# Attention on one Trainium2 core: the local heads' tiles move in between the steps of the branch and latent tiles, with two output banks open at a time

## The reference, cut to what matters

```python
h = rms_norm(x, g_pre);  projections = h @ w_in                 # 22 tiles of 128 columns
# 4 heads, three branches each, gated and added up:
o_a = g0 * attend(q, compressed k, v; 31 keys)                  # "cmp"
    + g1 * attend(q, selected k, v; causal)                     # "slc": all 8 blocks are chosen, so all earlier keys
    + g2 * attend(q, windowed k, v; causal, window 512)         # "win"
# 4 latent heads, query and key width 64 + 32 (rope), causal:
o_b = attend(q_full, k_full, v)                                 # "mla"
# 8 local heads, window 128, one key head, a sink in the softmax:
o_c = attend(q, k, v; window 128)                               # "swa"
mixed = concat(o_a, o_b, o_c) * silu(z)                         # 256 + 256 + 512 = 1024 columns: 8 tiles of 128
x = x + rms_norm(mixed @ w_out, g_post)
```

## Time and profile before

| | us |
|---|---|
| median of three runs (lowest to highest) | 2488.43 (2487.45 to 2489.74) |
| the profiled execution's own time | 2487.56 |
| its span in the profile | 2485.8 |
| PE busy in the span | 2422.5 (97%) |
| DVE busy | 1292.6 (52%) |
| ACT busy | 659.6 (27%) |
| POOL busy | 644.2 (26%) |
| first layer's steps on PE from step 3 to the output projection | 163.37 to 246.37 |
| the same in the second layer | 446.91 to 529.83 |

### The profile page before, as it was taken

How to read it: one execution, slowest core, us unless ns; L and a number is a source line. 1 busy time by engine, 2 the same in 40 slices (tenths; PEclk the granted TensorE clock), 3 DMA queues, 4 the chain that set the end, 5 groups by cost and what they waited for, 6 DMA issues and landing times. The chain is left out here.

```text
span 2485.8 us, 35391 instructions
## 1 busy us (share of the span) xinstructions
PE 2422.5 (97%) x13586; PEld 1982.0 (80%) x13586; DVE 1292.6 (52%) x1969; ACT 659.6 (27%) x1364; POOL 644.2 (26%) x509
## 2 busy tenths in 40 slices
PE   8999999999999999998999999999999998999997
PEld 6777777677888888887888888888888887888886
DVE  6558575665333446877333345333445967433344
ACT  3047311652111005443111103111104453211102
POOL 2027300463333111004333213333112004333211
PEclk9999999999999999999999999999999999999999
DMA  5210222012223321212222322223331202222322
GB/s 207 97 61 19 100 102 77 27 60 68 97 97 101 104 92 69 95 52 77 93 98 96 118 90 69 101 93 101 105 98 68 100 30 85 94 100 93 120 93 80
DMA packets 58144, 219.07 MB, mean 88 GB/s; under 512 B 6392, under 2 KB 9608, under 8 KB 57776
## 3 DMA queue, kind: packets, MB, share of 16 engines
q1 hardware_dynamic: 55312, 206.87, 24.4%
q10 hardware_dynamic: 2720, 10.66, 1.1%
HBM read 215.38 MB, written 2.13 MB: 87 GB/s over the span
## 5 line engine op out<-in xcount | busy, mean ns | idle before, releaser
L180 DVE CAST two_hi<-two_raw 128x1024 fp32r<-128x1024 f32 (+1 forms) x291 | 217.8, 748 | 891.9 <-PE bank L248 872.4
L241 PE MATMUL bank<-xh,two_hi 128*128 128x512 f32 x1712 | 425.8, 391 | 0.0
L244 PE MATMUL bank<-xh,two_lo 128*128 128x512 f32 x1712 | 423.0, 389 | 0.0
L248 PE MATMUL bank<-xl,two_hi 128*128 128x512 f32 x1712 | 422.9, 389 | 0.0
L182 DVE TENSOR_TENSOR two_lo<-two_raw,two_hi 128x1024 fp32r<-128x1024 f32 (+1 forms) x291 | 404.1, 1389 | 9.9
L244 PEld LDWEIGHTS bank<-xh,two_lo 128*128 128x128 f32 x1712 | 321.6, 188 | 66.7
L248 PEld LDWEIGHTS bank<-xl,two_hi 128*128 128x128 f32 x1712 | 321.6, 188 | 66.5
L241 PEld LDWEIGHTS bank<-xh,two_hi 128*128 128x128 f32 x1712 | 320.2, 188 | 67.3 <-issue 1.0
L1829 POOL TENSOR_TENSOR hm<-sg,hm 128x512 f32<-128x512 f32 x88 | 193.6, 2200 | 552.5 <-ACT hm L1806 552.5
L1806 ACT ACTIVATE hm<-bank 128x512 f32<-128x512 f32 x88 | 52.9, 601 | 416.1 <-PE bank L248 413.4
L241 PE MATMUL bank<-hh,two_hi 128*128 128x512 f32 x616 | 150.5, 392 | 0.0
(11 more groups left out here) (305 smaller groups left out, 3193.1 us busy)
## 6 DMA issues: line engine op xcount, KB each, us to landing
two_raw<-in_up SPq DMA_DIRECT2D x180, 512.0 KB, 3.2
two_raw<-in_down SPq DMA_DIRECT2D x64, 704.0 KB, 4.1
one_raw<-in_w_in SPq DMA_DIRECT2D x44, 512.0 KB, 3.2
two_raw<-in_w_in SPq DMA_DIRECT2D x40, 512.0 KB, 3.2
one_raw<-in_w_out SPq DMA_DIRECT2D x16, 512.0 KB, 3.2
two_raw<-in_w_out SPq DMA_DIRECT2D x16, 512.0 KB, 3.2
w<-in_w ACTq DMA_DIRECT2D x2, 2048.0 KB, 11.3
x<-in_x SPq DMA_DIRECT2D x4, 512.0 KB, 6.6
```

Source lines behind the costliest of these rows:

```text
L180: v.tensor_copy(st.hi[:, h, 0:w], st.raw[:, r, 0:w]).then_inc(st.hi_made, 1)
L241: pe.matmul(out[:], st.hi[:, slot, k * P:(k + 1) * P], xh[:, h * kp + k, :], start=h == 0 and k == 0, stop=False)
L244: pe.matmul(out[:], st.lo[:, slot, k * P:(k + 1) * P], xh[:, h * kp + k, :], start=False, stop=False)
L248: mm = pe.matmul(out[:], st.hi[:, slot, k * P:(k + 1) * P], xl[:, h * kp + k, :], start=False, stop=h == pieces - 1 and k == kp - 1)
```

## The change

```diff
-BRANCH_ORDER = (("cmp", 3), ("cmp", 2), ("slc", 3), ("win", 3), ("slc", 2), ("win", 2),
-                ("cmp", 1), ("cmp", 0), ("slc", 1), ("win", 1), ("slc", 0), ("win", 0))
+BRANCH_STEPS = ((("cmp", 3), ("cmp", 2)), (("slc", 3),), (("win", 3),), (("slc", 2),), "swa", (("win", 2),),
+                (("cmp", 1), ("cmp", 0)), "swa", (("slc", 1), ("win", 1)), (("slc", 0), ("win", 0)))
+LATENT_STEPS = ((("mla", 3),), "swa", (("mla", 2),), "swa", (("mla", 1), ("mla", 0)))
+WINDOWED_STEPS = ((("swa", 3), ("swa", 2)), (("swa", 1), ("swa", 0)))
 def attention_steps(pairs):
     steps = []
     for i, u in enumerate(pairs):
-        if steps and len(steps[-1]) == 1 and all(pairs[x]["width"] <= T // 2 and pairs[x]["tile"] == u["tile"]
-                                                 for x in (steps[-1][0], i)):
-            steps[-1] += (i,)
-        else:
-            steps.append((i,))
+        if u["step"] == len(steps):
+            steps.append(())
+        steps[-1] += (i,)
     return steps
 def attention_pairs():
...
+    pairs, count = [], 0
     for c in range(4):
-        for n in reversed(range(NT)):
-            add("swa", 4 + c, n, (2 * c, 2 * c + 1), first=True, last=True)
+        own = BRANCH_STEPS if c < 2 else LATENT_STEPS
+        windowed = iter(WINDOWED_STEPS)
+        for step in own:
+            tile = 4 + c if step == "swa" else c
+            members = next(windowed) if step == "swa" else step
+            for kind, n in members:
+                h = 2 * (c if kind == "swa" else c % 2)
+                u = dict(kind=kind, tile=tile, n=n, heads=(h, h + 1), step=count, first=True, last=True)
+                if kind in BRANCHES:
+                    u.update(branch=BRANCHES.index(kind), first=(kind, n) == own[0][0], last=(kind, n) == own[-1][-1])
+                pairs.append(u)
+            count += 1
...
-TILES = (0, 1, 2, 3, 4, 5, 6, 7)
+TILES = (4, 0, 5, 1, 6, 2, 7, 3)
...
-OUT_BANKS = (4, 7, 4, 7, 4, 7, 4, 7)
+OUT_BANKS = (7, 4, 4, 7, 7, 4, 4, 7)
...
     def is_scaled_by_v(i, hh):
+        if i in last_step:
+            return True
         if pairs[i]["kind"] == "swa":
-            return i in last_step or hh == 1 and i % 2 == 1
+            return hh == 1 and pairs[i]["n"] % 2 == 0
         return hh == 1 and pairs[i]["m"] > 2
...
                 for x in here(j - 2)[-1:]:
                     pe.wait_ge(s["logits"], 2 * (x + 1))
+                if i == first_of["swa"]:
+                    pe.wait_ge(s["taken"], N_IN)
```

More of the change, by code:

```diff
@@ L415, in attention_steps @@
     for i, u in enumerate(pairs):
-        if steps and len(steps[-1]) == 1 and all(pairs[x]["width"] <= T // 2 and pairs[x]["tile"] == u["tile"]
-                                                 for x in (steps[-1][0], i)):
-            steps[-1] += (i,)
-        else:
-            steps.append((i,))
+        if u["step"] == len(steps):
+            steps.append(())
+        steps[-1] += (i,)
     return steps
 def attention_pairs():
[L427 to L436, removed]
-        for n in reversed(range(NT)):
-            add("mla", 2 + c, n, (2 * c, 2 * c + 1), first=True, last=True)
-    for c in range(4):
-        for n in reversed(range(NT)):
-            add("swa", 4 + c, n, (2 * c, 2 * c + 1), first=True, last=True)
+    pairs, count = [], 0
+    for c in range(4):
+        own = BRANCH_STEPS if c < 2 else LATENT_STEPS
[10 more added lines that the diff above has]
+            count += 1
     for u in pairs:
```

## The result

| | before | after |
|---|---|---|
| median (lowest to highest), 6 runs each | 2488.48 us (2487.45 to 2490.14) | 2498.72 us (2495.53 to 2500.27) |
| the profiled execution's own time | 2487.56 | 2499.59 |
| a second profiled execution of after | | 2495.53 |

The ratio is 1.0038, with a 95% interval of 1.0028 to 1.0048: slower by about 10 us. In a second comparison on another occasion the same kernel gave 2496.94 (5 runs) and 1.0039 (1.0025 to 1.0054).

The account below looks back on a forecast made before the run. PE bounds the program (97% busy), idle about 4 us a layer in the steps. Terms 3.3 - 1.05 + 0.1 + 0.3 + 0.7 = +3.35 a layer, +6.7 for two: 2495.0 us, chance 0.55, own range 2491.5 to 2498, whole range 2488.9 to 2500.5.

Parts of the forecast that it names:

- splits: Splits behind steps 12 and 14 delay copies for PE's transposes: waits 1.7, 0.5 and 1.55 us, net +3.3 a layer.
- end of the stage: Before the output projection, ACT's conversions delay copies and last logits come later: +0.7 us a layer (-0.5 to +1.2).
- waits of the local stage: PE's waits in the eight local steps vanish once these have latent and branch neighbours: -1.05 us a layer.
- start: First transposes: the 0.93 us wait stays, DVE has four readings before its next copy: +0.1 us (0 to +0.3).
- small waits elsewhere: Steps 7 to 10 and 17 to 19, waits for ACT's copies behind local steps: +0.3 us a layer (0 to +0.6).
- PE's busy time: In the attention's steps, no PE product is added or removed; busy us stay the same within 0.3.
- Rival 1: Steps 12 to 16: splits absorbed after all, stalls shrink to about 0.4 us; 0 in all, 2488.5 us; chance 0.22.
- the banks: Each tile's first `weigh` comes at least one step after the gate product freeing its bank: cost 0.
- Rival 2: Whole stage: mixing gives DVE and ACT slack that absorbs the splits; -3.1 us a layer, 2482.2 us; chance 0.06.
- Rival 3: Port shared by DVE and POOL: each of four splits takes 0.97 us more, +3.9, 2498.9 us; chance 0.14.
- the signs named: Waits of 1.2 to 2.2 us in steps 14 and 16, none over 0.3 in 20 to 28, busy time within 0.3.

Follow-up runs that it names:

- the latent half: Kernel before with all four local tiles between and behind the latent steps, branch steps and splits unchanged: 2488.85 us, ratio 1.0004 to before.
- The control: The changed kernel, unaltered, run again beside the kernel before on one chip: 2496.94 us, ratio 1.0039 to before.
- the branch half: Changed kernel with only tiles 4 and 5 among branch steps, latent tiles and tiles 6 and 7 as before: 2495.71 us, ratio 1.0030 to before.

## Where the prediction was right and where not

The figures are us a layer at full clock, in the second layer. The splits' term is what leaving them out took away; the next four are differences of PE's idle time, and the last of PE's busy time, between after without splits and before (their two profiles, 84.17 and 82.92).

| term | predicted | measured |
|---|---|---|
| splits | +3.3 | +2.8 |
| end of the stage | +0.7 | +0.65 |
| waits of the local stage | -1.05 | -1.1 |
| start | +0.1 | -0.2 |
| small waits elsewhere | +0.3 | +0.8 |
| PE's busy time | 0 | +1.1 |
| sum | +3.35 | +4.05 |
| two layers | +6.7 | +8.0 |
| granted clock | none | 0 to +2 |

**The splits: right, in place, kind and size.** I counted PE wanting the transposes at 5.65 and getting them at 7.35 after its start of step 12; in the trace it got them at 7.83 (195.71 less 187.88), 1.60 late. The second stall was to end at 14.55 and ended at 14.68, 1.56 long, with 1.55 forecast. The first was to begin at 5.65 and began at 6.23: PE and DVE were both half a microsecond later than I counted. What was too dear is the +0.5 between them: no wait of over 0.15 us stands there. One reading behind it was wrong in a detail. The first of the transposes at 192.51 need ACT's copy, which ended at 192.36; DVE's, ended at 192.69, is needed only by the second three. So before had some 0.2 us to spare, not none. Rival 1, that the splits are absorbed, fell: they are absorbed in before and not in after.

**The reason, sharper than I had it.** The prediction named two things for the old order: the lightness of DVE's step behind the first split, and PE's own full steps. The second split shows that the first of them isn't enough. DVE's four readings of step 15 (slc0+win0) take as long, 0.98 us, as the two of 384 columns ahead of which a split costs 1.60 in the new order; but PE has the logits of mla3 (1.98 us) to do meanwhile. Counted from the start of the split on DVE, both sides can be read for every place that was tried:

| split behind | PE comes to the transposes two steps on | the copies are there | PE waits |
|---|---|---|---|
| 12, old order | 3.45 | 3.3 | 0 |
| 14, old | 4.18 | 3.5 | 0 |
| 9, old | 3.21 | 4.53 | 1.32 |
| 11, old | 3.13 | 5.23 | 2.10 |
| 12, new | 2.74 | 4.34 | 1.60 |
| 14, new | 2.72 | 4.28 | 1.56 |
| 15, new | 3.11 | 3.39 | 0.28 |
| 19, new | 4.13 | 4.96 | 0.83 |
| 21, new | 3.18 | 4.77 | 1.59 |
| 24, new | 4.47 | 4.68 | 0.21 |

(Where PE waited, the third column is the start of its transposes; in the first two rows it is the end of the last copy that they need first. The rows of 9, 11 and 15 are of the second layer.) The third column is 3.3 to 3.5 ahead of steps of 31 and 128 columns, and 4.3 to 5.2 ahead of 384 and 512; the second is long where PE has wide logits and full sums. Behind 19 and behind 24 comes the same mla3. Of the 0.62 us between their waits, 0.34 are on PE's side, whose sums are 8 passes in the one step and 16 in the other, and 0.28 on the other side, where the subtraction took 1.47 against 1.23. This table was read afterwards; no run changed PE's side alone.

**The end: right.** I wrote that two conversions stand before the third-last copy and four behind it; that is the order in the trace, with the wait of 0.82 at the four. The two end waits of the earlier trace rows, 0.51 and 0.62, became 0.73 and 0.82, with 0.21 and 0.18 beside them: 1.94 us, against 1.29 with the 0.16 that stood behind the two in before. Spreading the conversions gave back 0.87, which is more than the term, since it also does away with a wait that before has.

**The steps that failed are PE's busy time, put at nothing, and the small waits, put at +0.3.** The local stage's 1.05 us did vanish where I said: no idle entry of 0.3 us or more stands in steps 20 to 28. But the time came back elsewhere. I had held PE's busy time fixed within 0.3, and it grew by 1.08 (79.95 against 78.87), and by 1.12 without splits (79.99). The small waits came to +0.8, a large part of it in entries below 0.15 us. The transposes in the groups by shape, second layer of before (columns as in the earlier trace rows):

```profile
L1102 PE MATMUL bank<-k,lg_ring 128*128 128x128 f32 x160 | 22.8, 279 | 2.9 <-ACT pt_ring L867 1.5 <-POOL lg_ring L776 1.1 <-POOL lg_ring L775 0.2
```

And in the second layer of the second profiled execution of after:

```profile
L1103 PE MATMUL bank<-k,lg_ring 128*128 128x128 f32 x160 | 23.6, 279 | 6.2 <-ACT pt_ring L868 3.7 <-POOL lg_ring L776 1.6 <-DVE lg_ring L777 0.2
```

160 transposes of the same mean of 279 ns cover 23.6 us in place of 22.8: they overlap less, so PE stops for a moment within a group, and the view counts that as busy. In after without splits five such groups are 0.18 to 0.34 us longer than the shortest of their like, 1.26 us in all; in before without splits one is, by 0.23. The timeline of all engines shows one, behind a local step: four transposes take 0.96 us where 0.66 is usual, for the weight loads of the last two start 0.55 after those of the first two, when ACT's copy at 502.24 has ended (502.81). The row names no releaser, but by the kernel these two wait for that copy:

```profile
502.24 0.57 ACT L868 ACTIVATE pt_ring<-bank 128x512 f32<-128x512 f32 x1
502.38 0.20 PEld L1106 LDWEIGHTS bank<-k,lg_ring 128*128 128x128 f32 x2 [0.53 <-POOL lg_ring L777]
502.41 0.96 PE L1106 MATMUL bank<-k,lg_ring 128*128 128x128 f32 x4
...
502.93 0.20 PEld L1106 LDWEIGHTS bank<-k,lg_ring 128*128 128x128 f32 x2 [0.35 <-issue]
```

That copy stands behind the exponentials of a local step. Of the other four I can say only that they stand near local steps; what holds each was not tested. What was tested is the balance. With only the latent half (same branch steps as before) the stage is 82.98: the 1.05 taken out of the local steps is paid back in full even where no split is near, by the 0.50 among the latent steps, 0.30 more at the end and 0.36 of busy time.

**Small points.** The start: 0.93 became 0.71, better than the +0.1. No `weigh` waited for a gate product, so the banks cost 0 as said. Rival 2 fell. Rival 3, the port, was not seen in after: the subtractions took 1.23 and 1.22, since POOL did nothing at that time. With the split behind step 19 they did meet, and it took 1.47, +0.24, far from the +0.97 of the rival. What the rival had not seen is that here mostly POOL loses: its four scalings took 3.76 us there and 2.16 without a split. In before, four scalings of 31 columns took 2.85 us beside the second split (from 193.65), and 1.49 with the splits moved away (at 199.55), while the subtraction took 1.27. The Trainium skill's page "SBUF — State Buffer", section "Who interferes with whom", says that the engine which issues first holds the shared port for its whole instruction while the other is blocked. By that rule a subtraction could lose up to one undisturbed scaling, 0.54 us (an estimate: a quarter of 2.16), and the 0.24 is within it. The four scalings lost 1.60 in all, a little more than one subtraction takes; whether the cast before it holds them too, no run separates.

**The median.** The median of before stands 0.9 above its profiled execution, so 8.0 us more make 2496.5. The control gave 2496.94, the first comparison 2498.72. Of the 3.7 us between that and the forecast of 2495.0, 1.3 are the terms and some 0.2 rounding; about 2.2 I put down to the granted clock, which the prediction took for unchanged. That part is argued from the profiled executions, not shown for each run. Both medians lie inside the range of 2488.9 to 2500.5; the first is 0.7 above the forecast's own 2498 and beside rival 3's 2498.9, though its mechanism was not there. The nearness is partly luck: the splits were 0.5 a layer too dear, and the busy time and small waits 1.6 too cheap. Of the signs named, all came but one, the busy time of PE the same within 0.3.

## What to carry to other kernels

A long piece of work between two steps of an engine is hidden if the engine that needs what comes behind it has enough of its own to do until then. So when steps are reordered, look first, for each such piece, at what now follows it on both engines; here moving two pieces alone was worth 2.3 to 2.9 us a layer, in either order. Where all engines work near their limit, evening out one stage moves its waits rather than removing them, and a part of them hides in the bound engine's busy time: compare the busy time of the same instructions, not only the idle entries. And one conversion block in front of a wanted copy is cheap to divide.

## What the runs showed of the hardware that I had not expected

TensorE's granted clock sometimes fell shortly after such waits, which are little longer than a microsecond. Windows of the first layer of after, first profiled execution, around the two waits (194.1 to 195.7 and 201.0 to 202.6):

```profile
196.00:200.00 4.00, 3.91 (x40) 2.74 (x39) 3.93 (x15) 3.04 (x10) 0.88 (x1) 1.00 0.07 22
200.00:204.00 4.00, 2.44 (x24) 1.86 (x22) 3.43 (x20) 3.21 (x13) 2.65 (x3) 0.85 0.39 131
204.00:208.00 4.00, 4.00 (x36) 3.27 (x36) 1.65 (x9) 0.85 (x6) 0.95 (x3) 0.72 0.00 0
208.00:212.00 4.00, 3.78 (x44) 2.68 (x41) 2.62 (x17) 3.95 (x15) 2.60 (x6) 1.00 0.02 4
```

Before the fall PE had worked 2.44 of 4 us. In 204 to 208 it is busy throughout at 0.72, part of the time at 1.2 GHz in place of 2.4; 16 products of `weigh` take 1.97 us there, against 1.09. The stage lost 1.57 us by it. In the second layer, with the same waits, the clock stayed at 1.00. Before with moved splits, second layer, after its wait of 2.10 us:

```profile
480.00:484.00 4.00, 2.43 (x14) 2.13 (x16) 2.77 (x16) 3.38 (x14) 1.73 (x2) 0.55 0.29 110
484.00:488.00 4.00, 4.00 (x28) 2.83 (x24) 0.69 (x4) 0.00 (x0) 0.00 (x0) 0.59 0.00 0
```

In the profiled executions 5 of the 14 stages with a wait of 1.5 us or more ran below full clock (the first of after, both of before with moved splits, the second of after with spread conversions, the first of the branch half), and none of the 12 others.

But such falls are not peculiar to these waits. Every profiled execution has six or more outside the stages, before too, at 0.83 in 90 to 100 us, 290 to 300, 370 to 380, 580 to 590 and others. At the first of these no idle time of PE is shown; it worked through 32 passes of 31 columns (88.47 to 92.25) and had 4.00 of 4 us busy:

```profile
90.00:94.00 4.00, 4.00 (x25) 3.62 (x25) 1.29 (x2) 0.22 (x1) 0.00 (x0) 0.73 0.36 131
```

So the mean clock of a run says little about the stages. The profiled execution with splits behind 21 and 24 had 0.990 and took 2495.05 us, and both its stages ran at 1.00; that of after with spread conversions had 0.992, and its second stage fell. At a mean of 0.990 or below were 32 of 54 runs of kernels with a wait of 1.5 us or more in the stages, and 25 of 126 of the others, 11 of 73 for before itself. Of before the runs at 0.990 took some 1.5 us more than those at 0.992. So long waits and a lower clock go together, but loosely: after with spread conversions, two long waits, had 2 of 11, and with splits behind 19 and 24, none so long, 6 of 11. One theory was that the fall wants two long waits close together. The two stages profiled with one split moved ran at 1.00, as did the two with splits behind 21 and 24, but 6 of 9 runs of the first had 0.990; whether those fell in the stages is not known. What decides whether the clock falls stays open, and that it makes the spread of after, 4.7 us over six runs against 2.7 for before, is likely but not shown.
